# Two last mixers: matmuls on constants ahead of the first turned head, and VectorE's maximum of the next head ahead of the division

## The chip, the cores and the metric

The kernel runs on one NeuronCore of a Trainium2 chip. Its engines work side by side: TensorE (PE) multiplies, with weight loads shown apart (PEld), VectorE (DVE) and ScalarE (ACT) work elementwise, GpSimd (POOL) does some of that too and issues a few transfers, and SyncE (SP) issues the rest. The metric is the device time of one launch in microseconds (us). The time before is 1626.62 us, the median of three runs (1623.18 to 1626.62). The execution that was profiled took 1630.73 us, and its span from the first to the last instruction is 1628.8 us.

## The reference, cut to what matters

The program is two residual blocks on 256 tokens of width 1024, in float32. The first block has feed-forward parts and two mixers. The second block has two layers, and each is one mixer. These two are the "last mixers".

```python
for l in range(2):                                   # second_block
    h = rms_norm(x, norm_g[l])
    q_a, k_a, v_a, q_h, f_h, i_h, q_m, z = split(h @ w_in[l])
    o_a = moba_attention(qa, ka, va)                 # 8 heads of 64, causal over 256 keys
    o_h = rms_norm(hgrn2_chunkwise(q_h, f_h, i_h))   # 4 heads of 128
    o_m = memory_attention(qm, km, vm)               # 4 heads of 128, all 256 memory keys
    x = x + concat([o_a, o_h, o_m]) * silu(z) @ w_out[l]
```

For a head, attention is `p = softmax(q k^T * scale)`, then `p v`. With 256 tokens in blocks of 256, the first attention is causal attention inside one block.

## The kernel before, in words

All weights come as panels of 2048 columns. ScalarE writes the upper part of a panel (L1499), VectorE the rest (L1814), and TensorE multiplies the parts in three products, which together keep float32's accuracy. Small products of activations (attention, norms) are plain float32 products.

The order of the work is not found by a scheduler. `order()` writes one list of steps, each with its engine, and every engine takes its own steps from that list in that order; each step starts with the semaphore waits that it needs. An engine never passes a step that waits. `merge` lays several chains of rounds side by side: round i of the list is round i of each chain, in the order of the chains. `rounds(steps, units)` makes a chain in which, in round r, each step works on the unit r minus its lag. `weave` puts panel products between rounds; in the attention rounds no panels are left, so that TensorE has only attention there.

`last_mixer(l)` is one of the two last mixers. Its attention chain has 12 heads: moba 0 to 7, then matt 0 to 3 (the memory heads). One head goes through seven steps:

1. `scores`, PE L1409 and L1411: q times k into a bank of PSUM. The moba heads have 64 channels, so these products use 64 rows of the array (64\*128 in a row of the profile); matt heads use 128.
2. `mask_max`, DVE L2101 (moba) or L2099 (matt): adds the mask, copies to `probs` (in `work`), finds the row maximum. It waits for `scores` of its head, and for `turn_p` two heads back, whose buffer it takes.
3. `exp`, ACT L1708 twice, each with a row that reads the sum.
4. `divide`, DVE L2114 and L2118: one over the sum, times the probabilities.
5. `turn_p`, PE L1421, L1422, L1427 (matt: L1424, L1425): transposes of 128 columns; waits for `divide`.
6. `p_cols`, ACT L1719: copies the transposed probabilities out of PSUM.
7. `attend`, PE L1367 and L1368: v times the probabilities.

In round r TensorE does `turn_p` of head r-2, `scores` of head r, `attend` of head r-3. ScalarE does `p_cols` of head r-2 and `exp` of head r. VectorE does, by the table `ATTEND`, `divide` of head r-1 and then `mask_max` of head r. A second table, `ATTEND_TWO`, is used by the attention of the first block's second mixer and has the two VectorE steps the other way round.

Rounds 0 and 1 also hold the last norms: L1396 is a product with a matrix of ones, L1697 and L1698 on ScalarE make the reciprocal root from it, L2065 on VectorE applies it. In the first of the two mixers ScalarE also computes row statistics of the memory input in round 5 (L1540 to L1548) and VectorE scales it (L1892). In the second, every other round from 2 to 8 has four transposes more (L1221). `y_splits` and the output panels follow.

Semaphores of `pe_done`, `act_done` and `dve_done` count finished steps; steps named in `UNCOUNTED` don't count.

Of the kernel before, what the change touches and what calls it, by code (L numbers as in the profile page):

```python
# [165 lines left out]
DOWNS = list(RESIDUALS.values())  # L166

LATE = {name: (BASE[name] + N_OF[name] + SLOTS - 1, min(BASE[name] + N_OF[name] + SLOTS, PANELS)) for name in DOWNS}
UNCOUNTED = {"half", "half_hi", "half_lo", "gate_first", "up_first", "first_hi", "first_lo", "ffn_down", "logs", "split_hi", "split_lo", "ffn", "panel", "load", "store"}
PAIRS = DC // 2  # L170

# [4 lines left out]
def rounds(steps, units):  # L177

    return [[(engine, kind, (units[r - lag],)) for engine, kind, lag in steps if 0 <= r - lag < len(units)]
            for r in range(len(units) + max(lag for _, _, lag in steps))]  # L180
# [6 lines left out]
def merge(*chains):  # L187

    return [sum((c[i] for c in chains if i < len(c)), []) for i in range(max(map(len, chains)))]

def weave(chain, pieces, places):

    out, rest = [], []
    pieces = sorted(zip(places, range(len(pieces)), pieces))
    for i, r in enumerate(chain):
        out += r + rest
        rest = []
        while pieces and pieces[0][0] <= i:  # L200
            out += rest
            first, *rest = pieces.pop(0)[2]
            out.append(first)
    return out + rest + sum((p[2] for p in pieces), [])

def halves(panels):

    out, late = [], []  # L210
    panels = panels[:-2] + [p[:2] for p in panels[-2:]]
    for (_, _, args), *rest in panels:
        now = [half_split(s, 0) if s[1] in HALVED else s for s in rest]
        out += [[("pe", "half", (*args, 0)), *late], [("pe", "half", (*args, 1)), *now]]
        late = [half_split(s, 1) for s in rest if s[1] in HALVED]
    out[-1] += late
    return out
# [5 lines left out]
def half_split(step, part):  # L223
# [7 lines left out]
ATTEND = [("pe", "turn_p", 2), ("pe", "scores", 0), ("pe", "attend", 3), ("act", "p_cols", 2), ("dve", "divide", 1),  # L231
          ("dve", "mask_max", 0), ("act", "exp", 0)]

ATTEND_TWO = ATTEND[:4] + [ATTEND[5], ATTEND[4], ATTEND[6]]
# [23 lines left out]
def square_sums(tag):  # L258

    return [("pool", "add", (tag, b)) for b in range(1, PAIRS)]  # L260
# [37 lines left out]
def panel_list(name, extra=None, start=0, stop=None):  # L298

    all_ = []  # L300
    for k in range(start, N_OF[name] if stop is None else stop):
        out = []
        all_.append(out)
        n = BASE[name] + k
        out.append(("pe", "panel", (name, k)))
        if not name.startswith("out"):
            out.append(("dve" if (name, k) in EVACUATED_BY_DVE else "act", "evacuate", (name, k)))
        late = LATE.get(name, (0, 0))
        if n + SLOTS < PANELS and not late[0] <= n + SLOTS < late[1]:

            out += splits(n + SLOTS)[:1 if n + SLOTS == late[0] - 1 else 2]
        out += (extra or {}).get(k, [])
    return all_
# [25 lines left out]
def ffn_steps(f):  # L339
    tag = f"ffn{f}"  # L340
    return norm_steps(tag) + ([("pe", "up_first", (f,)), ("pe", "norm_sum", (tag,))] if f == 0 else
                              [("pe", "gate_first", (f, b)) for b in range(PAIRS)] + [("pe", "norm_sum", (tag,)), ("pe", "up_first", (f,))]) + [("pe", "ffn", (f,)), ("act", "rstd", (tag,)), ("act", "ffn", (f,)), ("dve", "ffn", (f,))]
# [32 lines left out]
def hgrn_rounds(l):  # L375

    out = [[("dve", "f_abs", (l,)), ("act", "f_ln", (l,))], [("dve", "f_log", (l,))]]
    if l:
        out += [[("act", "f_ln2", (l,)), ("dve", "f_log2", (l,))]]
    out += [[("act", "k_gate", (l,)), ("dve", "cum_f", (l,))], [("pe", "diagonal", (l,)), ("dve", "diagonal_in", (l,))]]  # L380
    ahead = len(out)
    for r in range(8 + 2):
        out.append([(e, k, (l, v)) for e, k, v in
                    [("dve", "gap_f", r), ("act", "decay_f", r), ("dve", "q_level", r - 1), ("pool", "k_level", r - 1),
                     ("pe", "level", r - 2), ("dve", "level_in", r - 2)] if 0 <= v < 8])
    return out + [[("pe", "hgrn_out", (l, g)) for g in (0, 1)]], ahead

def last_mixer(l):

    hgrn, ahead = hgrn_rounds(l)
    hgrn[ahead + 9] += [("act", "silu", (f"in2_{l}", 15)), ("act", "logs", ())]
    n = ahead + 9
    qk = [(f"mq{l}", 0), (f"mk{l}", 0), (f"mq{l}", 1), (f"mk{l}", 1)]
    h = n + 7
    chains = [rounds(NORM_COLS, [(f"sk{l}", 0), (f"sk{l}", 1)]), hgrn,
              [[]] * n + rounds(NORM_COLS, qk + [(f"ho{l}", 0), (f"ho{l}", 1), (f"sq{l}", 0), (f"sq{l}", 1)]),
              [[]] * (n + 2) + rounds(ROPE, qk),
              [[]] * (h + 11) + [[("dve", "gate_out", ((f"moba{l}", g),)) for g in (0, 1)]],
              [[]] * h + rounds(ATTEND, [(f"moba{l}", i) for i in range(8)] + [(f"matt{l}", i) for i in range(4)]),  # L400
              [[]] * (h + 13) + [y_splits(l, 0), y_splits(l, 2)]]
    if l == 0:
        load, *stats = mem_norm(1)
        chains += [[[]] * (h + 1) + [[load]] + [[]] * 3 + [[s for s in stats if s[0] == "act"]] +
                   [[s for s in stats if s[1] == "scale"]]]
    if l:
        chains += [[[]] * (h + 2) + sum(([[("pe", "turn_back", (b,)), ("act", "rows_back", (b,))], []] for b in range(PAIRS)), [])]
    places = [n + r for r in BESIDE_2]
    out = weave(merge(*chains), halves(panel_list(f"in2_{l}", None, 4)), places)
    return (out + late_splits(f"in2_{l}") + [("dve", "gate_out", ((f"matt{l}", g),)) for g in (0, 1)]  # L410
            + y_splits(l, 8) + y_splits(l, 10))

def late_splits(name):

    n = BASE[name] + N_OF[name]
    return splits(n + 1, n + 2)

def y_splits(l, b):  # L420
    return [("act", "y_hi", (l, b)), ("dve", "y_lo", (l, b))]
# [10 lines left out]
def mem_norm(l):  # L432

    tag = f"mem{l}"
    return [("pool", "load", (tag,))] + row_stats(tag, 0) + row_stats(tag, 1) + \
        [("dve", "scale", (tag, t)) for t in (0, 1)] + [("pe", "turn_x", (tag, b)) for b in range(PAIRS)]
# [11 lines left out]
def order():  # L448
# [8 lines left out]
    out += square_sums("ffn0") + [("pool", "load", ("tab1",)), ("act", "wab_hi", ()), ("dve", "wab_lo", ())]  # L457
    out += [s for s in ffn_steps(0) if s[1] in UNCOUNTED or s[1] in ("norm_sum", "rstd")] + ffn_tail(0, "mix0")

# [62 lines left out]
for _e, _k, _a in ORDER:  # L522
    if _k not in UNCOUNTED:
        _counts[_e] = _counts.get(_e, 0) + 1
# [4 lines left out]
def at(engine, kind, *args):  # L529

    return COUNT_AT[engine, kind, args]

def build(nc, x_in, mem_in, pos_in, panels, gains, small_in, tab0, tab1, tab2, tab3, out):
    with ExitStack() as ctx:
        def sb(name, shape, dt=F32):
            return ctx.enter_context(nc.sbuf_tensor(name, shape, dt))

        def sem(name):
            return ctx.enter_context(nc.semaphore(name))  # L540
# [14 lines left out]
        const = sb("const", [P, tab0.shape[1]])  # L555
# [6 lines left out]
        ps = ctx.enter_context(nc.psum_tensor("ps", [P, 8, 512], F32))  # L562
# [6 lines left out]
        def cst(name):  # L569
            a, n = PLACES[0][name]  # L570
            return const[:, a:a + n]
# [104 lines left out]
        pe_done, act_done, dve_done, pool_done = (done[e] for e in ("pe", "act", "dve", "pool"))  # L676
# [6 lines left out]
        first_hi, first_lo = sem("first_hi"), sem("first_lo")  # L683
# [30 lines left out]
        for g in range(2):  # L714
            s2 = slice(2 * g, 2 * g + 2)
            s4 = slice(4 + 2 * g, 6 + 2 * g)
            ones, ones64 = cst("ones"), cst("ones64")
# [285 lines left out]
        def _(pe):  # L1003
# [426 lines left out]
            def attend(unit):  # L1430
# [7 lines left out]
                p = p_t[:, i % 2]  # L1438
                weighted(o, v[:, 0], v[:, 1], p[:, 0:SEQ], p[:, SEQ:512] if full else p[:, SEQ:384], full).then_inc(pe_done, 1)

            def lam_sum():
                pe.wait_ge(dve_done, at("dve", "lam_mul"))
                pe.matmul(ps[:, 3, 0:2], cst("ones")[0:64, :], lam_c[0:64, 0:2], start=True, stop=True).then_inc(pe_done, 1)
# [20 lines left out]
            def hgrn_out(l, g):  # L1464
                pe.wait_ge(dve_done, at("dve", "level_in", l, 7))
                for i in range(2):
# [10 lines left out]
                         "turn_m": turn_m, "kq": kq, "double_y": double_y, "double": double, "u": u, "state": state_mm,  # L1477
                         "from_state": from_state, "delta_out": delta_out, "ret_scores": ret_scores, "ret_out": ret_out,
                         "swap": swap, "cn_sum": cn_sum, "scores": scores, "turn_p": turn_p, "attend": attend,
                         "lam_sum": lam_sum, "diagonal": diagonal, "level": level, "hgrn_out": hgrn_out})  # L1480

        @block.scalar
# [831 lines left out]
```

## Time and profile before

| | us |
|---|---|
| median of three runs | 1626.62 |
| the profiled execution | 1630.73 |
| its span | 1628.8 |
| TensorE busy | 1552.1 (95% of the span) |
| VectorE busy | 1177.2 (72%) |
| ScalarE busy | 769.3 (47%) |
| chain that ended last: PE, DVE, ACT | 78%, 13%, 6% |

### The profile page before, as it was taken

The numbers are of one execution on the slowest core, as the hardware profiler recorded it, in microseconds if no ns is written. First come the engines' busy times: TensorE is split into PE (matmuls) and PEld (weight loads), VectorE is DVE, ScalarE is ACT, GpSimd is POOL, SyncE is SP. The second block draws the span as 40 slices with busy tenths as digits, with TensorE's granted clock in tenths as the row PEclk, the third lists the DMA queues.
The fourth block names the chain that finished last, engine by engine and source line by source line (L and its number), as shares of the span: only waits on it lengthen the run. The fifth ranks groups of instructions, "written<-read, shape, count | busy, mean of one in ns | idle before, by whom it ended". The sixth has DMA issues, their size and how long they took to land.

```text
span 1628.8 us, 23944 instructions
## 1 busy us (share of the span) xinstructions
PE 1552.1 (95%) x9974; PEld 1380.3 (85%) x9974; DVE 1177.2 (72%) x1391; ACT 769.3 (47%) x943; POOL 94.3 (6%) x66
## 2 busy tenths in 40 slices
PE   7999998998999999999998999999999899899998
PEld 6888898887888888888987888888999579799757
DVE  7888667636887788786676787867787565589644
ACT  5433545325433454335535534355656554554643
POOL 1000000010000000000000100001031001012000
PEclk9999989999999999999999999999999799999969
DMA  7555533204555545555421555544543124434202
GB/s 275 194 197 181 180 128 132 78 27 160 202 186 185 184 174 193 195 181 181 181 104 68 214 184 186 192 169 151 181 156 119 63 104 168 144 130 148 86 1 78
DMA packets 51888, 246.76 MB, mean 151 GB/s; under 512 B 4619, under 2 KB 5771, under 8 KB 27718
## 3 DMA queue, kind: packets, MB, share of 16 engines
q1 hardware_dynamic: 50662, 238.29, 41.2%
q0 software_dynamic: 1120, 6.96, 1.2%
q8 instruction: 79, 1.29, 0.3%
q14 instruction: 27, 0.22, 0.0%
HBM read 244.18 MB, written 1.05 MB: 151 GB/s over the span
## 4 chain that ended last, share of the span: by engine, by line
PE 78%; DVE 13%; ACT 6%; issue 3%; DMA 0%; SPq 0%; DVEq 0%; POOL 0%; ACTq 0%
PE ps L1055 19%; PE ps L1057 10%; PE ps L1006 9%; PE ps L1007 9%; PE ps L1008 9%; PE ps L1107 7%; PE ps L1252 4%; PE ps L1108 4%; DVE w_lo L1814 3%; ACT w_hi L1499 2%; DVE act_two L1920 1%; PE ps L1367 1%; PE ps L1396 1%; PE ps L1411 1%; ACT act_two L1577 1%
## 5 line engine op out<-in xcount | busy, mean ns | idle before, releaser
L1499 ACT ACTIVATE w_hi<-raw 128x2048 fp32r<-128x2048 f32 x188 | 359.2, 1914 | 390.3 <-PE ps L1057 278.3
L1814 DVE TENSOR_TENSOR w_lo<-raw,w_hi 128x2048 fp32r<-128x2048 f32 x188 | 437.2, 2331 | 144.4 <-ACT w_hi L1499 141.4
L1055 PE MATMUL ps<-act_two,w_hi 128*128 128x512 f32 x1408 | 445.1, 398 | 5.0 <-DVE w_lo L1814 2.4
L1006 PE MATMUL ps<-act_two,w_hi 128*128 128x256 f32 x1120 | 329.7, 294 | 16.8 <-DVE act_two L1920 5.4
L1007 PE MATMUL ps<-act_two,w_hi 128*128 128x256 f32 x1120 | 320.2, 286 | 0.0
L1008 PE MATMUL ps<-act_two,w_lo 128*128 128x256 f32 x1120 | 320.2, 286 | 0.0
L1057 PEld LDWEIGHTS ps<-act_two,w_lo 128*128 128x128 f32 x1408 | 265.9, 189 | 63.1
L1057 PE MATMUL ps<-act_two,w_lo 128*128 128x256 f32 x1408 | 277.8, 279 | 0.0
L1006 PEld LDWEIGHTS ps<-act_two,w_hi 128*128 128x128 f32 x1120 | 218.3, 195 | 23.5 <-issue 7.8
L1055 PEld LDWEIGHTS ps<-act_two,w_hi 128*128 128x128 f32 x1408 | 215.4, 189 | 8.0 <-DVE w_lo L1814 3.6
L1007 PEld LDWEIGHTS ps<-act_two,w_hi 128*128 128x128 f32 x1120 | 218.3, 195 | 3.2 <-issue 3.1
L1008 PEld LDWEIGHTS ps<-act_two,w_lo 128*128 128x128 f32 x1120 | 218.2, 195 | 0.0
L1107 PE MATMUL ps<-g_two,w_hi 128*128 128x512 f32 x384 | 135.6, 396 | 0.0
L1107 PE MATMUL ps<-act_two,w_hi 128*128 128x512 f32 x320 | 112.9, 397 | 2.8 <-DVE act_two L1853 2.8
L1797 DVE TENSOR_TENSOR w_lo<-raw,w_hi 128x1024 fp32r<-128x1024 f32 x72 | 99.0, 1403 | 21.7 <-ACT w_hi L1508 20.5
L1006 PE MATMUL ps<-w_hi,act_two 128*128 128x256 f32 (+1 forms) x336 | 107.7, 321 | 0.0
L1108 PE MATMUL ps<-g_two,w_lo 128*128 128x256 f32 x384 | 107.1, 279 | 0.0
L1007 PE MATMUL ps<-w_lo,act_two 128*128 128x256 f32 (+1 forms) x336 | 101.5, 302 | 0.0
L1008 PE MATMUL ps<-w_hi,act_two 128*128 128x256 f32 (+1 forms) x336 | 101.5, 302 | 0.0
L990 POOL TENSOR_TENSOR pair<-pair 128x512 f32<-128x512 f32 x27 | 41.2, 1528 | 872.9 <-ACT pair L1556 872.2
L1108 PE MATMUL ps<-act_two,w_lo 128*128 128x256 f32 x320 | 89.3, 279 | 0.0
L1107 PEld LDWEIGHTS ps<-g_two,w_hi 128*128 128x128 f32 x384 | 72.1, 188 | 16.6
(282 smaller groups left out, 2079.0 us busy)
## 6 DMA issues: line engine op xcount, KB each, us to landing
raw<-panels SPq DMA_DIRECT2D x184, 1024.0 KB, 4.8
raw<-panels SPq DMA_DIRECT2D x80, 512.0 KB, 4.8
raw<-panels SPq DMA_DIRECT2D x8, 256.0 KB, 5.7
table<-tab POOLq DMA_DIRECT2D x1, 1472.0 KB, 9.4
table<-tab POOLq DMA_DIRECT2D x1, 1216.0 KB, 5.5
xn<-x_in SPq DMA_DIRECT2D x4, 256.0 KB, 4.8
work<-mem_in POOLq DMA_DIRECT2D x1, 1024.0 KB, 9.3
xn<-mem_in POOLq DMA_DIRECT2D x1, 1024.0 KB, 5.2
```

The lines of the kernel that those rows point to most:

```text
L990: nc.gpsimd.tensor_tensor(pair[:, 0:512], pair[:, 0:512], pair[:, 512 * b:512 * b + 512], ALU.add).then_inc(pool_done, 1)
L1006: pe.matmul(o, l[0], r[0], start=start, stop=False, skip_group_check=shared)
L1007: pe.matmul(o, l[0], r[1], start=False, stop=False, skip_group_check=shared)
L1008: return pe.matmul(o, l[1], r[0], start=False, stop=stop, skip_group_check=shared)
L1055: pe.matmul(grid(ps[:, bank + half], 2), w[half][0], act_two[:, slots[c]], start=c == 0, stop=False)
L1057: ins = pe.matmul(ps[:, bank + half, 0:SEQ], w[half][1], act_hi[:, slots[c]], start=False, stop=c == DC - 1)
L1107: pe.matmul(grid(ps[:, bank], 2), hi, two, start=first and m == 0, stop=False)
L1108: ins = pe.matmul(ps[:, bank, 0:SEQ], lo, two[:, 0], start=False, stop=last and m == len(quarters) - 1)
L1252: ins = pe.transpose(oh, lhs(h), ident) if turn else pe.matmul(oh, lhs(h), rhs(h), start=True, stop=True)
L1499: nc.scalar.activation(w_hi[:, s], raw[:, s], ACT.Copy).then_inc(panel_hi, 1)
L1797: ins = tt(w_lo[:, s, c], raw[:, s, c], w_hi[:, s, c].bitcast(F32), ALU.subtract)
L1814: tt(w_lo[:, s], raw[:, s], w_hi[:, s].bitcast(F32), ALU.subtract).then_inc(panel_lo, 1)
```

## The change

Two things are changed in `last_mixer`, so in both last mixers.

The attention rounds take `ATTEND_TWO` in place of `ATTEND`. On VectorE, `mask_max` of head r now stands ahead of `divide` of head r-1.

A new TensorE step `keep_busy(l, 14)` stands at the end of round 1, behind `scores` of moba 1 and ahead of `turn_p` of moba 0. It waits for the rope of the last keys, which has read bank 3 of PSUM, and then multiplies a matrix of ones with 384 columns of constants 14 times into bank 3. Nobody reads the result, and the step has no semaphore of its own.

```diff
-UNCOUNTED = {"half", "half_hi", ...
+UNCOUNTED = {"keep_busy", "half", "half_hi", ...
@@ last_mixer(l)
-              [[]] * h + rounds(ATTEND, [(f"moba{l}", i) for i in range(8)] + [(f"matt{l}", i) for i in range(4)]),
-              [[]] * (h + 13) + [y_splits(l, 0), y_splits(l, 2)]]
+              [[]] * h + rounds(ATTEND_TWO, [(f"moba{l}", i) for i in range(8)] + [(f"matt{l}", i) for i in range(4)]),
+              [[]] * (h + 13) + [y_splits(l, 0), y_splits(l, 2)],
+              [[]] * (h + 1) + [[("pe", "keep_busy", (l, 14))]]]
@@ the steps of TensorE
+            def keep_busy(l, n):
+
+                pe.wait_ge(dve_done, at("dve", "rope", (f"mk{l}", 1)))
+                for _ in range(n):
+                    pe.matmul(ps[:, 3, 0:384], cst("ones"), const[:, 0:384], start=True, stop=True)
```

TensorE in the first last mixer, from the norm product of round 1 on. Before:

```order
L1396 MATMUL ps<-pair,const 128x512
L1409 MATMUL ps<-work 128x128
L1411 MATMUL ps<-work 128x256
L1421 MATMUL ps<-const,work 128x128
L1422 MATMUL ps<-const,work 128x128
L1427 MATMUL ps<-const,work 128x128
L1409 MATMUL ps<-work 128x128
L1411 MATMUL ps<-work 128x256
```

The same place in the changed kernel, whose lines are 1 higher up to L1441 of before and 7 higher behind it:

```order
L1397 MATMUL ps<-pair,const 128x512
L1410 MATMUL ps<-work 128x128
L1412 MATMUL ps<-work 128x256
L1446 MATMUL ps<-const 128x384 x14
L1422 MATMUL ps<-const,work 128x128
L1423 MATMUL ps<-const,work 128x128
L1428 MATMUL ps<-const,work 128x128
L1410 MATMUL ps<-work 128x128
L1412 MATMUL ps<-work 128x256
```

The 14 products (L1446) have come between the scores of head 1 and the three transposes of head 0; nothing else has moved on TensorE.

VectorE in the first last mixer, from the norm of round 1 on: the division of head 0 (L2114, L2118) and the maximum of head 1 (L2101, with the rows that read its result), then the same for the next pair. Before:

```order
L2065 SCALAR_TENSOR_TENSOR work<-work,small,pair 128x512
L2114 RECIPROCAL stat<-stat 128x2
L2118 TENSOR_SCALAR work<-work,stat 128x128
L2118 TENSOR_SCALAR work<-work,stat 128x256
L2101 ISA work,stat<-ps,table 128x128
L2101 ISA stat 128x1
L2101 ISA work,stat<-ps,table 128x256
L2101 ISA stat 128x1
L2114 RECIPROCAL stat<-stat 128x2
```

The same place now:

```order
L2072 SCALAR_TENSOR_TENSOR work<-work,small,pair 128x512
L2108 ISA work,stat<-ps,table 128x128
L2108 ISA stat 128x1
L2108 ISA work,stat<-ps,table 128x256
L2108 ISA stat 128x1
L2121 RECIPROCAL stat<-stat 128x2
L2125 TENSOR_SCALAR work<-work,stat 128x128
L2125 TENSOR_SCALAR work<-work,stat 128x256
L2108 ISA work,stat<-ps,table 128x128
```

The maximum of head r has moved in front of the division of head r-1, in every round of both mixers. ScalarE's order is as it was.

## Rows read from the trace of the kernel before

**Rows 1.** The profile page: TensorE's granted clock in 40 slices, in tenths.
```profile
PEclk9999989999999999999999999999999799999969
```

**Rows 2.** Stretch table: length, busy PE, PEld, DVE, ACT, POOL, granted clock, DMA.
```profile
1278.43:1283.47 5.04, 0.15 (x1) 0.00 (x0) 1.80 (x7) 2.79 (x7) 0.00 (x0) 0.67 0.47 185
1289.95:1305.49 15.54, 15.54 (x45) 8.70 (x44) 6.32 (x27) 9.29 (x32) 0.00 (x0) 0.50 0.00 1
1305.49:1308.59 3.10, 3.10 (x12) 2.18 (x12) 1.86 (x10) 1.48 (x5) 0.00 (x0) 0.68 0.00 0
857.00:863.60 6.60, 6.33 (x27) 5.17 (x28) 4.25 (x16) 4.30 (x14) 0.00 (x0) 0.50 0.20 82
877.65:881.15 3.50, 1.86 (x11) 1.56 (x11) 2.02 (x12) 2.37 (x8) 0.00 (x0) 1.00 0.00 0
1556.88:1574.11 17.23, 17.23 (x53) 10.41 (x53) 5.44 (x28) 7.11 (x23) 0.00 (x0) 0.50 0.00 1
```

**Rows 3.** Timeline, first mixer, where TensorE stands idle: start, length, engine, line.
```profile
1277.99 0.59 PE L1411 MATMUL ps<-work 64*128 64x256 f32 x2
1281.88 0.75 DVE L2065 SCALAR_TENSOR_TENSOR work<-work,small,pair 128x512 f32<-128x512 f32 x1 [3.13 <-ACT pair L1698]
1282.67 0.17 DVE L2114 RECIPROCAL stat<-stat 128x2 f32<-128x2 f32 x1
1283.47 0.47 PE L1421 MATMUL ps<-const,work 128*128 128x128 f32 x1 [4.89 <-DVE work L2118]
```

**Rows 4.** Timeline of TensorE: two fp32 products of 512 columns at full clock.
```profile
1252.71 1.02 PE L1396 MATMUL ps<-pair,const 128*128 128x512 f32 x2
1253.57 1.02 PE L1385 MATMUL ps<-work,table 128*128 128x512 f32 x2
```

**Rows 5.** Timeline, first mixer: one round of an early head at half clock.
```profile
1289.95 0.48 PE L1421 MATMUL ps<-const,work 128*128 128x128 f32 x1
1290.50 0.17 DVE L2114 RECIPROCAL stat<-stat 128x2 f32<-128x2 f32 x1 [1.17 <-ACTq L1711]
1290.70 0.55 DVE L2118 TENSOR_SCALAR work<-work,stat 128x128 f32<-128x128 f32 x2
1292.36 1.11 PE L1367 MATMUL ps<-work 128*64 128x256 f32 x2
1292.56 0.29 DVE L2101 CUSTOM_DVE_ANT_0 work<-ps,table 128x128 f32<-128x128 f32 x1 [1.32 <-issue]
```

**Rows 6.** Timeline, layer 1 mixer of the first block: one round at full clock.
```profile
877.65 0.33 PE L1421 MATMUL ps<-const,work 128*128 128x128 f32 x1 [1.65 <-DVE work L2118]
878.69 0.59 PE L1367 MATMUL ps<-work 128*128 128x256 f32 x2
878.99 0.29 DVE L2101 CUSTOM_DVE_ANT_0 work<-ps,table 128x128 f32<-128x128 f32 x1 [1.39 <-PE ps L1411]
881.15 0.33 PE L1421 MATMUL ps<-const,work 128*128 128x128 f32 x1 [1.65 <-DVE work L2118]
```

**Rows 7.** Timeline, first mixer: the last heads, at full clock.
```profile
1313.90 0.33 PE L1421 MATMUL ps<-const,work 128*128 128x128 f32 x1 [0.59 <-DVE work L2118]
1314.82 0.59 PE L1411 MATMUL ps<-work 128*128 128x256 f32 x2
1317.81 0.51 ACT L1708 ACTIVATE work<-work,stat 128x256 f32<-128x256 f32 x1 [1.25 <-DVE work L2099]
1320.11 0.33 PE L1421 MATMUL ps<-const,work 128*128 128x128 f32 x1 [1.45 <-DVE work L2118]
```

**Rows 8.** Timeline of ScalarE, first mixer: the row statistics, first and last.
```profile
1298.23 0.63 ACT L1540 ACTIVATE work<-xn 128x512 f32<-128x512 f32 x1
1303.09 0.20 ACT L1548 ACTIVATE stat<-stat 128x1 f32<-128x1 f32 x1
```

**Rows 9.** Timeline of TensorE, second mixer: the first and last turned head.
```profile
1549.74 0.48 PE L1421 MATMUL ps<-const,work 128*128 128x128 f32 x1 [4.89 <-DVE work L2118]
1588.68 0.33 PE L1421 MATMUL ps<-const,work 128*128 128x128 f32 x1 [1.26 <-DVE work L2118]
```

More of the change, by code:

```diff
@@ L168 @@
 LATE = {name: (BASE[name] + N_OF[name] + SLOTS - 1, min(BASE[name] + N_OF[name] + SLOTS, PANELS)) for name in DOWNS}
-UNCOUNTED = {"half", "half_hi", "half_lo", "gate_first", "up_first", "first_hi", "first_lo", "ffn_down", "logs", "split_hi", "split_lo", "ffn", "panel", "load", "store"}
+UNCOUNTED = {"keep_busy", "half", "half_hi", "half_lo", "gate_first", "up_first", "first_hi", "first_lo", "ffn_down", "logs", "split_hi", "split_lo", "ffn", "panel", "load", "store"}
 PAIRS = DC // 2
@@ L1479, in _ @@
                          "swap": swap, "cn_sum": cn_sum, "scores": scores, "turn_p": turn_p, "attend": attend,
-                         "lam_sum": lam_sum, "diagonal": diagonal, "level": level, "hgrn_out": hgrn_out})
+                         "lam_sum": lam_sum, "keep_busy": keep_busy, "diagonal": diagonal, "level": level, "hgrn_out": hgrn_out})
         @block.scalar
```

## The prediction

> **What bounds the kernel now.** I read the granted clock of the page first. Two slices near the ends of the layers fall to 7 tenths and 6 tenths [rows 1]; these are the attention rounds of the two last mixers. Then the table by stretch. In the first mixer TensorE stands idle in 1278.43:1283.47 (0.15 us busy of 5.04) and the mean clock of that stretch is 0.67, so that it falls in there. It stays at 0.50 for the four rounds of 1289.95:1305.49, in which TensorE has no idle time at all, and comes back inside 1305.49:1308.59 [rows 2]. The second mixer does the same: idle for 4.89 us up to 1549.74 [rows 9], 0.50 in the four rounds of 1556.88:1574.11 [rows 2]. Outside these holes TensorE is the bound, and all that follows a mixer waits for it, so each us won or lost here is one of the total.
>
> Third, the timeline says why TensorE idles. The scores of head 1 start their last product at 1277.99. The first transpose waits for the division of head 0, which waits on VectorE behind the norm L2065 at 1281.88, which waits for ScalarE's norm (3.13 us) [rows 3]. I call the starts of L1421 turns T0 to T11, one per head. In the first mixer T0 is 1283.47, T2 1289.95, T6 1305.49, T7 1308.59, T11 1320.11.
>
> **The constants.** A float32 product of 512 columns takes 1253.57 - 1252.71 = 0.86 us at full clock [rows 4], so 384 columns take 0.645 and 14 of them 9.03 us. They start when the scores of head 1 are through: 1277.99 + 0.43 (256 columns) = 1278.42. They end at 1287.45. T0 was 1283.47, so they run 4.0 us past the hole that they fill. The hole of the second mixer has the same length, so T0 is late by 4.0 there too. Bounds for the 14: the row shows two records for one product; were only one of them needed, the 14 would take 4.5 us, VectorE would set the end (below) and T0 be late by 0.65. If they ran at half clock they would take 18 us and T0 be late by 13. I take 9.03, as the row is a product of the same type and the same size of weights, at full clock. Their wait, for a rope long done, costs nothing.
>
> In the meantime VectorE does the maximum of head 1 (0.68, from 1282.67) and then divides head 0 (0.75: 1290.50 to 1290.70 + 0.55 [rows 5]), so T0 could be at 1284.15. The 0.65 us by which the new order alone makes T0 late is hidden by the constants; without them it would show.
>
> **The new order of VectorE.** Before, a head's exp, division and the next maximum were a loop. Now the maximum of head r is made while exp works on head r-1. But it has to wait for the scores of head r, and these stand on TensorE behind turn r-2. So the new loop is turn, scores, maximum, division, next turn. At half clock: turn and scores 1292.36 - 1289.95 = 2.41, to VectorE's start 0.20, maximum 0.68, division 0.75, to the next turn 0.05: 4.1 us [rows 5]. Before, four rounds took 15.54 us [rows 2], 3.9 each, bound by TensorE. At full clock: 1.04 for turn and scores, 0.30 to VectorE [rows 6], and again 0.68 + 0.75 + 0.05: 2.8 us. The first block's mixer, which has this order already, confirms the loop: its round in rows 6 is 3.50 us, and it has one multiplication of 0.68 more in front of its division. So the reorder costs 0.2 a round where the clock is low and it cannot get a round under 2.8 where it is high.
>
> **Does the clock hold?** This decides the size. The constants keep TensorE at work from 1278.4 to 1287.5, so it is at full clock when the turns begin. What comes then is a round with a turn and scores but no attend, and then rounds of 2.8 us in which TensorE has about 1.7 us of work (1.04 of rows 6, and 0.65 for an attend of as many columns as the scores) and idles for the rest. The nearest rows speak both ways. For holding: the round of rows 6 (1.86 us busy of 3.50) stays at 1.00 [rows 2]. Against: in that round all products use 128 rows, while a moba head's scores use 64 [rows 3]. And in 1289.95:1305.49 TensorE was busy without a gap with exactly these turns, scores and attends, and the clock did not come back; panel products brought it back within 857.00:863.60, and it came back in the very round in which the first 128-row scores stand [rows 2]. So the moba rounds weigh little, and at full clock they fill only 60% of the time, less than they did while the clock stayed low. Just ahead of the fall TensorE also had 64-row scores and one norm product, and then nothing. I take it that the clock falls again, 2.5 to 6 us behind the constants, in both mixers.
>
> **The sum.** Turns of the first mixer: T0 +4.0. T0 to T2 was 6.48 and is now one full round and one in between (2.8 + 3.45 = 6.25): -0.2. T2 to T6, four rounds at half clock: 16.4 against 15.54: +0.85. T6 to T11, with matt scores of twice 256 columns: T6 to T7 was 3.10; the loop (scores end later, maximum 0.82, division 0.75) makes it 4.2. The next is 3.2, and two rounds at full clock are each 1315.25 - 1313.90 = 1.35 to the end of the scores, + 0.30 + 0.82 + 0.85 = 3.3 [rows 7]; VectorE's two times are for 256 columns, estimated from the 0.68 and 0.75 above. The last turn gains: its maximum and exp are made early, so that it follows the one before by 2.30 (1317.81 to 1320.11 [rows 7]) less 0.86 of lead, 1.45. Together 4.2 + 3.2 + 6.6 + 1.45 = 15.5 against 14.62: +0.9. First mixer: +5.5.
>
> Second mixer: T0 +4.0; T0 to T2 was 7.14, is 6.25: -0.9; T2 to T6 was 17.23 [rows 2], of which two rounds carry four transposes more and stay bound by TensorE, the other two +0.2 each: +0.4; T6 to T11 was 1588.68 - 1574.11 = 14.57 and is 15.5: +0.9. Second mixer: +4.4. Sum +9.9 us on the profiled execution's 1630.73, whose span is 1628.8. The median is 4 us below that execution, and the difference carries over: 1626.62 + 9.9 = 1636.5.
>
> **Rivals.** (a) The clock holds in both mixers. Then T0 to T6 is six rounds of 2.8. In the first mixer ScalarE's row statistics (1298.23 to 1303.29, 5.0 us [rows 8]) stand between the exps of heads 5 and 6 and no longer hide: +2.0. T6 = 1287.45 + 16.8 + 2.0 = 1306.3, then 3.2 + 3.2 + 6.6 + 1.45: T11 = 1320.8, +0.6. In the second: 1553.7 + 16.8 + 14.45 = 1585.0, -3.7. Sum -3.1: 1623.5. For it speaks the 1.00 of rows 6's round; against it the half-height scores. The Trainium skill, in "TensorE: Matmul & The Clock Gate", section "Why this matters for your kernels", advises that no long idle gap be left between bursts of matmuls if the clock is to stay up. By that rule alone this rival would come true, since the changed kernel leaves only short gaps; no run here shows yet whether short gaps between small products suffice, and the four half-clock rounds without any gap make me doubt it.
> (b) The clock holds in one mixer or falls several rounds later. Each round spared saves 1.3 us of loop and up to 2 in the second mixer: the total is then near 1631.
> (c) The change works as a wait only: the constants are at full clock, but the fall comes at once when they end, and then T0 to T2 is 8 us. That is +1.8 and +1.0 more: 1639. It decides the sign by itself from the point where the constants outlast the hole by more than the rounds give back.
> (d) The constants are cheap, the change is the reorder alone: the clock falls in the hole as before, +0.65 + 0.85 + 0.9 and +0.65 + 0.4 + 0.9: about +4, 1631.
>
> **How the numbers follow.** Forecast 0.6, (a) 0.14, (b) 0.12, (c) 0.1, (d) 0.04. The likeliest's own range is 1632 to 1641 (the place of the fall, +-1.5 a mixer, and the loop's length). The range for 8 in 10 takes in most of (b) and a part of (a): 1625.5 to 1641.5. About 0.2%, 3.3 us, is what a measurement of this kernel can tell from no change: faster needs 1623.3 or less, half of (a) with its uncertainty, 0.08. Within 0.2% are the other half and a third of (b): 0.14. Slower: 0.78.
>
> **What would show it.** L1446's 14 products at 0.64 us each, from 1278.4 to 1287.5, clock 1.00 over them; then a fall to 0.50 within two or three turns and a rise again with the matt scores. Turns 2.8 us apart at full clock and 4.1 at half, with VectorE's maximum always right behind the scores and its division right behind the maximum. T11 at 1326 in the first mixer. I am wrong if the granted clock is 1.00 through the turns of either mixer, or if turns at full clock come under 2.6 us apart, which would mean that the scores do not stand in the loop.

## The result, and the profile after

The changed kernel takes 1631.61 us (median of nine runs, 1629.36 to 1635.96), the kernel before 1625.02 in the same comparison (nine runs, 1621.44 to 1627.66). The ratio is 1.0043, with a 95% interval of 1.0029 to 1.0056: 7.0 us slower, 4.7 to 9.1. The profiled execution of the changed kernel took 1633.33 us. Its granted clock, against [rows 1]:

```profile
span 1631.4 us, 24056 instructions
PEclk9999999999999999999998999999999899999999
```

The slice of the first last mixer has gone from 7 to 8 tenths, that of the second from 6 to 9. So the constants did what they are named for in one mixer, and yet the time rose. The table by stretch of the changed kernel says where (length, busy PE, PEld, DVE, ACT, POOL, granted clock, DMA):

```profile
1286.99:1291.00 4.01, 2.39 (x15) 1.59 (x13) 1.36 (x7) 1.94 (x6) 0.00 (x0) 0.99 0.00 0
1291.00:1311.50 20.50, 19.75 (x56) 11.15 (x55) 8.31 (x37) 11.37 (x40) 0.00 (x0) 0.50 0.00 0
1549.04:1558.69 9.65, 9.65 (x32) 5.56 (x31) 2.83 (x13) 3.78 (x11) 0.00 (x0) 1.00 0.00 0
1558.69:1561.91 3.22, 1.93 (x12) 1.19 (x10) 1.45 (x7) 1.29 (x5) 0.00 (x0) 1.00 0.01 3
1561.91:1576.98 15.07, 12.12 (x63) 7.29 (x64) 6.80 (x35) 8.85 (x30) 0.00 (x0) 1.00 0.00 1
```

In the first mixer the first turn (transposes of head 0) comes at 1286.99, and 4.0 us later the clock is at 0.50, for 20.5 us. In the second the same 9.65 us pass between the scores of head 1 and the first turn, and the clock then stays at 1.00 through all turns (the last two rows above show it up to T6). The timeline of the first mixer answers to [rows 3]: VectorE has long divided head 0 when the constants end.

```profile
1277.34 0.59 PE L1412 MATMUL ps<-work 64*128 64x256 f32 x2
1277.86 9.30 PE L1446 MATMUL ps<-const 128*128 128x384 f32 x28
1282.01 0.29 DVE L2108 CUSTOM_DVE_ANT_0 work<-ps,table 128x128 f32<-128x128 f32 x1
1282.69 0.17 DVE L2121 RECIPROCAL stat<-stat 128x2 f32<-128x2 f32 x1
1286.99 0.27 PE L1422 MATMUL ps<-const,work 128*128 128x128 f32 x1
```

The 14 products run from 1277.86 to 1286.99, 9.13 us; the division starts at 1282.69, so that head 0 waits some 3.5 us for nothing. One round of the second mixer, at full clock, answers to [rows 6]:

```profile
1561.91 0.33 PE L1422 MATMUL ps<-const,work 128*128 128x128 f32 x1 [1.29 <-DVE work L2125]
1563.24 0.65 PE L1368 MATMUL ps<-work 128*64 128x256 f32 x2
1563.44 0.29 DVE L2108 CUSTOM_DVE_ANT_0 work<-ps,table 128x128 f32<-128x128 f32 x1 [1.58 <-PE ps L1412]
1564.12 0.17 DVE L2121 RECIPROCAL stat<-stat 128x2 f32<-128x2 f32 x1
1564.93 0.33 PE L1422 MATMUL ps<-const,work 128*128 128x128 f32 x1 [0.82 <-DVE work L2125]
```

Turn, scores, maximum, division, turn: 3.02 us. TensorE idles before each turn until the division is done. The line L1368 is the first product of `attend`, so its start marks where the scores end.

To compare mixers I count from the start of the last scores product of head 1, so that what happened earlier in the launch falls out. T0 and T11 are the first and last turns, counted in us from that point. The eleven numbers behind them are the distances from each turn to the next. All are differences of starts in the timelines of TensorE:

```
kernel, mixer        T0     T11    distances
before, 1           5.48  42.12   2.60 3.88 3.88 3.88 3.88 3.90 3.10 2.40 2.91 3.29 2.92
before, 2           5.48  44.42   3.32 3.82 4.79 3.83 4.79 3.82 4.05 2.08 2.42 3.29 2.73
after, 1            9.65  47.59   2.96 3.27 4.10 4.10 4.10 4.10 4.03 3.21 3.32 3.32 1.43
after, 2            9.65  42.31   3.22 3.02 3.01 3.01 3.02 3.01 3.15 3.21 3.32 3.33 1.36
```

From the last turn of one mixer to the scores of the next, 224.1 us pass in both kernels, and 40.1 from the last turn of the second to the end. What the change does lies in the mixers alone. The stretch ahead of them, whose code is the same, has no fixed length: over the twelve profiled runs of this document the scores of head 1 start between 1272.29 and 1281.38 us. On the whole the later starts go with more time at half clock on the way there, 17 to 38 us in all (from the granted clock read in steps of 1 us). So one profiled run can differ from another by more than this change is worth before the changed code begins.

### The profile page after: what moved, and what is told of

Its sections match the earlier page's. It is cut to its first block, busy times and chain, and to the rows that moved or that the text cites. A ratio compares the mean times of both kernels' runs of the same rounds, so it can differ in the third digit from the quotient of the medians.

```text
span 1631.4 us, 24056 instructions
## 1 busy us (share of the span) xinstructions
PE 1556.9 (95%) x10030; PEld 1381.7 (85%) x10030; DVE 1177.0 (72%) x1391; ACT 768.2 (47%) x943; POOL 94.3 (6%) x66
## 4 chain that ended last, share of the span: by engine, by line
PE 77%; DVE 13%; ACT 4%; issue 3%; DVEq 0%; POOL 0%; ACTq 0%
PE ps L1056 18%; PE ps L1058 9%; PE ps L1007 9%; PE ps L1009 9%; PE ps L1008 9%; PE ps L1108 7%; PE ps L1253 4%; PE ps L1109 4%; DVE w_lo L1821 3%; ACT w_hi L1506 2%; DVE act_two L1927 1%; PE ps L1446 1%; PE ps L1397 1%; PE ps L1412 1%; ACT act_two L1584 1%
```

## The experiments

**The kernel before, once more.** The ratio says 7 us, but the two profiles differ by 2.6. No edit, one profiled run.

> The kernel before, looked at once more. Theory A (the first profile was an execution with a longer stretch at half clock than most): the stretches at half clock in the two last mixers are shorter by 3 to 7 us each, the turns before and after them are the same, the time is 1622 to 1627 us. Rival: stretches as in the first profile (27.3 and 30.7 us), and the difference lies ahead of the last mixers.

It took 1624.42 us. First mixer: T11 at 42.08, as in the first profile. Second: T11 at 42.02 in place of 44.42, since the clock came back after 23.9 us and not 30.7. The half-clock stretch of this run ends inside the second row:

```profile
1545.85:1561.40 15.55, 15.55 (x48) 9.66 (x48) 6.09 (x32) 7.37 (x24) 0.00 (x0) 0.50 0.00 1
1561.40:1582.39 20.99, 18.17 (x86) 12.12 (x84) 11.05 (x47) 11.68 (x37) 0.00 (x0) 0.88 0.00 1
```

The rest of the difference lies ahead of the last mixers: the scores of head 1 start at 1274.18 and not at 1277.99, with less time at half clock near 212 us (3.4 against 10.2). So each expectation was half right. The first profile is of an execution near the slow end of its kernel, and times should be compared by medians, stretches by counting from a point inside.

**The changed kernel, once more.** No edit, one profiled run.

> The changed kernel, looked at once more. Theory A (where the clock falls behind the constants is decided anew in each run): the two mixers need not do as in the first profile; a mixer in which it holds has turns 3.0 us apart, T11 at 42.3 us from the last scores product of head 1 in the second mixer and about 44 in the first (with ScalarE's row statistics in the way), one in which it falls has 4.1 between turns. Rival D (something in the first mixer alone makes it fall, each time): it falls in the first and holds in the second again.

It took 1632.87 us. Its stretches:

```profile
1284.91:1287.90 2.99, 1.37 (x9) 0.81 (x7) 1.36 (x7) 1.33 (x5) 0.00 (x0) 1.00 0.00 0
1287.90:1311.80 23.90, 23.16 (x65) 13.06 (x66) 9.05 (x41) 11.97 (x42) 0.00 (x0) 0.50 0.00 0
1561.00:1567.80 6.80, 6.50 (x22) 3.98 (x20) 2.71 (x14) 2.76 (x10) 0.00 (x0) 0.50 0.00 0
1567.80:1590.88 23.08, 18.14 (x95) 11.73 (x93) 12.41 (x54) 12.81 (x39) 0.00 (x0) 1.00 0.01 1
```

The first mixer fell 3 us behind the constants (T11 at 48.70), the second fell too, but for 6.8 us only (T11 at 44.30). So whether and where the clock falls differs from run to run. The mean clock of the changed kernel's nine runs also splits them, though it doesn't say in which mixer the clock fell: four at 0.980 to 0.983 take 1631.6 to 1636.0 us, five at 0.986 to 0.988 take 1629.4 to 1632.2. Even the second group is slower than the median before.

With two profiled runs of each kernel, T11 moves by +5.5 and +6.6 us in the first mixer and by nothing on average in the second (42.31 and 44.30 against 44.42 and 42.02). That makes 6 of the 7 us. Two runs of each are few, so this is a match in size and not a proof.

**The two halves apart.** The new order alone:

```diff
-              [[]] * (h + 13) + [y_splits(l, 0), y_splits(l, 2)],
-              [[]] * (h + 1) + [[("pe", "keep_busy", (l, 14))]]]
+              [[]] * (h + 13) + [y_splits(l, 0), y_splits(l, 2)]]
```

> Maximum ahead of the division in both last mixers, no constants. Turns are counted from the start of the last scores product of head 1 (5.48 us to T0 and 42.1 us to T11 before, in the first mixer). Theory A (the reorder costs by itself: its loop goes through the scores): the clock falls in the hole as before, T0 comes 0.65 us later, rounds at half clock are 4.1 us in place of 3.9, the last turns cost 0.9 more: about +2 us a mixer, +4 in all. Rival B (the reorder is what pays or is free, and the constants carry the whole loss): 0 or less.

1634.61 us against 1626.25: ratio 1.0058 (1.004 to 1.0077), 9 us slower, where +4 was expected. The sign went to theory A. The size was missed in the first two rounds:

```profile
1282.86 0.47 PE L1421 MATMUL ps<-const,work 128*128 128x128 f32 x1 [5.57 <-DVE work L2124]
1285.47 0.29 DVE L2107 CUSTOM_DVE_ANT_0 work<-ps,table 128x128 f32<-128x128 f32 x1 [2.67 <-PE ps L1411]
1286.15 0.17 DVE L2120 RECIPROCAL stat<-stat 128x2 f32<-128x2 f32 x1
1286.95 0.48 PE L1421 MATMUL ps<-const,work 128*128 128x128 f32 x1 [1.62 <-DVE work L2124]
```

At half clock the new loop is 4.10 us in each of the first six rounds of the first mixer, also in the first two, which took 2.60 and 3.88 before, as no attend bounds them yet. In the second mixer the first two take 4.35 and 4.10, where they took 3.32 and 3.82. T0 is at 6.17, 0.69 later. T11 is at 46.15 and 45.81: +4.0 and +1.4 against the first profile of before, +4.1 and +3.8 against the second. On average that is 6.6 us; where the other 2 to 3 us of the measured 9 lie, the profiled run doesn't show.

The constants alone:

```diff
-              [[]] * h + rounds(ATTEND_TWO, ...
+              [[]] * h + rounds(ATTEND, ...
```

> The 14 products of constants, with the old order of VectorE. T0 is 4.2 us late in both mixers as in the changed kernel. Theory A: where the clock holds, rounds are bound by exp, division, maximum (2.6 us, as the first round before the change) and not by 3.0; so this is 2 to 4 us faster than the changed kernel in each mixer where the clock holds, and 2 faster where it falls (rounds of 3.9, the cheaper tail). Against before: near 0 with the clock held in both, +4 if it falls in one. Rival B: slower than the changed kernel, since the reorder is lost.

1623.92 us: ratio 0.9985 (0.9972 to 0.9998), 2.4 faster than before. T0 is at 9.65, but the turns that follow are 1.27, 2.82, 2.60, 2.60, 2.60 us apart in the first mixer, and 1.77, then 2.3 to 2.6 in the second. One such round:

```profile
1288.28 0.33 PE L1422 MATMUL ps<-const,work 128*128 128x128 f32 x1 [0.63 <-DVE work L2125]
1288.94 0.40 ACT L1715 ACTIVATE work<-work,stat 128x128 f32<-128x128 f32 x1 [0.94 <-DVE stat L2108]
1290.07 0.17 DVE L2121 RECIPROCAL stat<-stat 128x2 f32<-128x2 f32 x1 [1.17 <-ACTq L1718]
1290.86 0.29 DVE L2108 CUSTOM_DVE_ANT_0 work<-ps,table 128x128 f32<-128x128 f32 x1
1290.88 0.33 PE L1422 MATMUL ps<-const,work 128*128 128x128 f32 x1 [0.41 <-DVE work L2125]
```

The loop of the old order is exp, division, maximum: 2.60 us at full clock against 3.01 with the new order. T11 is at 42.55 and 38.54. In the first mixer the clock held up to ScalarE's row statistics, where one turn came 6.42 us after the one before and the clock fell for some 3.4 us. In the second it held throughout:

```profile
1550.85:1579.74 28.89, 24.52 (x133) 16.20 (x131) 15.79 (x72) 17.96 (x55) 0.00 (x0) 1.00 0.00 1
```

That makes a clean pair. The second mixer of the changed kernel's first profile also has T0 at 9.65 and the clock at 1.00 through all turns, and its T11 is at 42.31. The two differ by the order on VectorE alone, with the clock out of play, and the new order costs 3.8 us there.

**Fewer constants.** With the new order, and with the old:

```diff
-              [[]] * (h + 1) + [[("pe", "keep_busy", (l, 14))]]]
+              [[]] * (h + 1) + [[("pe", "keep_busy", (l, 8))]]]
```

> The changed kernel with 8 products of constants in place of 14: 5.2 us, which is the length of the hole. Theory A: T0 is only 0.65 us late (set by VectorE's new order), 3.5 us a mixer better than the changed kernel, as long as the clock holds as there: 7 us faster in all, about as fast as before or up to 4 faster. If the clock falls in both mixers, as in the kernel before: +4 against before, as the reorder alone. Rival C (the constants' length does not cost, since the engines behind are the bound): equal to the changed kernel.

1630.18 us, ratio 1.0029 (1.0016 to 1.0042): 4.7 slower than before, and some 2 faster than the changed kernel, not 7. The two intervals overlap, so even the 2 are not sure. T0 is at 6.16 as expected, 3.5 us earlier. But the clock falls in the first mixer behind the second turn, in the second mixer for 6.8 us from 1561.0, and T11 is at 44.14 and 41.04:

```profile
1291.40:1311.80 20.40, 19.66 (x57) 11.03 (x56) 8.31 (x37) 11.56 (x40) 0.00 (x0) 0.50 0.00 0
1561.00:1567.80 6.80, 6.06 (x22) 3.70 (x20) 2.32 (x12) 3.10 (x11) 0.00 (x0) 0.50 0.00 0
```

The comparison with the changed kernel goes over two sets of runs and is only as good as their common kernel before. Trace and medians don't agree well here. By the two T11 together this profiled run is 6.3 us better than the changed kernel's two on average, near the 7 expected, and level with before (85.2 against 86.5 and 84.1). The median is 4.7 above before all the same. The profiled run is one of the slowest (1632.64), and it is late ahead of the mixers, with the scores of head 1 at 1281.38. What makes the other runs slow stays open. Rival C fell in the trace, where 3.5 us of T0 come off in each mixer; the medians confirm it in the pair with the old order, below.

> 8 products of constants with the old order of VectorE. Theory A: T0 as before (+0.1), rounds of 2.6 us at full clock where it holds. If it holds in both mixers: first mixer about -3, second about -8 against before, 10 us faster in all; if it falls in both behind the constants: -2. Rival C: equal to the constants alone with 14.

1617.93 us, ratio 0.9956 (0.9941 to 0.9972): 7.2 faster than before. T0 at 5.79, T11 at 39.85 and 35.51, turns 2.6 us apart; the clock held but for 6.8 us behind the row statistics in the first mixer:

```profile
1280.97:1297.90 16.93, 11.50 (x59) 6.76 (x57) 7.86 (x38) 11.12 (x39) 0.00 (x0) 1.00 0.00 0
1297.90:1304.70 6.80, 6.19 (x18) 3.85 (x19) 3.60 (x15) 4.26 (x15) 0.00 (x0) 0.50 0.00 0
```

Against the 14 with the old order the eight are 4.8 us faster, and the intervals (0.9941 to 0.9972, 0.9972 to 0.9998) no more than touch. With the new order the same eight constants give 12 us less. This pair differs by the reorder alone, the fall of the clock that came with it included (it fell in both mixers with the new order, in one with the old), and it is the largest single effect of the study. The other two pairs say nearly the same: the new order costs 9 us without constants, and 9 with 14 of them (+7.0 against -2.4).

**Does the clock fall because the rounds are thin?** One more product in each of the rounds 2 to 8 of the first mixer, in a bank that is free there:

```diff
-              [[]] * (h + 1) + [[("pe", "keep_busy", (l, 14))]]]
+              [[]] * (h + 1) + [[("pe", "keep_busy", (l, 14))]] + [[("pe", "keep_busy", (l, 1))]] * (0 if l else 7)]
-                    pe.matmul(ps[:, 3, 0:384], cst("ones"), ...
+                    pe.matmul(ps[:, 3 if n > 1 else 5, 0:384], cst("ones"), ...
```

> The changed kernel, and in the first mixer one product of constants (0.65 us) more at the end of each of the rounds 2 to 8, where TensorE waits for the division at full clock. Theory A (the clock falls there because the rounds behind the constants hold too little work): it holds in the first mixer in nearly all runs, turns stay 3.0 us apart but for the 5 us of row statistics, T11 at 43 to 45 us in place of 47.6; 3 us faster than the changed kernel at its lower clock, and the runs no longer fall into two groups. Rival F (the fall has another cause, or one more product delays each turn): the clock falls as before and the first mixer takes 4 us more.

```profile
1284.09:1300.80 16.71, 15.63 (x69) 8.25 (x67) 7.55 (x36) 9.59 (x32) 0.00 (x0) 1.00 0.00 0
1300.80:1318.26 17.46, 13.34 (x63) 8.27 (x63) 10.45 (x41) 10.25 (x33) 0.00 (x0) 1.00 0.00 1
```

The clock holds from the first turn to the last. Turns are 3.01 apart, one of 4.72 carries the row statistics, and T11 is at 43.83 in place of 47.6 and 48.7. In the second mixer, which has no such products, it held too (T11 at 42.30). The mean clock of all seven runs is 0.985 to 0.990: one group, where the changed kernel had two. 1628.92 us, ratio 1.0037 (1.0021 to 1.0052), against 1.0043 for the changed kernel. The 3 us that were expected between the two can't be told from none.

So in the profiled run more work in those rounds went with a clock that stayed up, at no cost to the turns, and the kernel is still slower than before. With the clock at full level through both mixers, T0 is late by 4.2 us and the loop is the longer one. That explains only a part: T11 of the two mixers together is 0.8 us later than in the two profiles of before on average, while the ratio says 6 us. The profiled run is the fastest of its seven (1626.65), and what the others lost is not shown.

**The row statistics.** Eight constants, old order, ScalarE's six steps in six rounds:

```diff
-        chains += [[[]] * (h + 1) + [[load]] + [[]] * 3 + [[s for s in stats if s[0] == "act"]] +
-                   [[s for s in stats if s[1] == "scale"]]]
+        a, d = [s for s in stats if s[0] == "act"], [s for s in stats if s[1] == "scale"]
+        chains += [[[]] * (h + 1) + [[load]] + [[]] * 3 +
+                   [[a[0]], [a[1]], [a[2]], [a[3], d[0]], [a[4]], [a[5]], [d[1]]]]
```

> Eight constants and the old order, and in the first mixer ScalarE's row statistics are spread over the rounds 5 to 10, a step each, in place of one block behind the exp of head 5. Theory A: the turn that took 6.42 us takes 2.6 to 3.4, some 3 us less with 0.5 to 1 given back in the later rounds, and the clock no longer falls behind it: 2 to 4 us faster than the eight constants with the block, 10 to 12 faster than before. Rival E (ScalarE's work is only moved and each round grows by it, since exp is in the loop): the same time as with the block.

1612.5 us, ratio 0.9937 (0.9916 to 0.9958): 10 us faster than before, as expected, and 3 more than with the block, though the intervals overlap. The eight runs fall into two groups: five at 1609.6 to 1612.9 us with mean clock 0.989 to 0.992, three at 1618.8 to 1619.6 with 0.980 to 0.982. The profile is of the second group: the clock fell at 1286.0, 4.0 us behind the first turn, and T11 of the first mixer is at 40.94. The turn that took 6.42 us takes 3.88, at half clock.

```profile
1282.00:1286.00 4.00, 3.05 (x17) 1.90 (x16) 1.68 (x9) 2.46 (x9) 0.00 (x0) 1.00 0.00 0
1286.00:1306.50 20.50, 20.45 (x60) 11.49 (x59) 8.85 (x43) 10.47 (x36) 0.00 (x0) 0.50 0.00 0
```

**A version that beats both.** The same with one product more a round in the first mixer (the edit of the thin rounds, with 8 in place of 14):

> Eight constants, old order, row statistics spread, and in the first mixer one product of constants more at the end of each of the rounds 2 to 8. Theory A (the runs of the kernel without these products fall into two groups, near 1612 and near 1619 us, by whether the clock falls behind the eight constants): all runs in the faster group, turns of the first mixer 2.6 us apart, T11 at 36 to 37 us from the last scores product of head 1, median 1609 to 1613. Rival F (the product delays each turn, or the clock falls for another reason): two groups again, or turns 3.2 us apart and 1616.

1611.43 us, ratio 0.9914 (0.9898 to 0.993): 14 us faster than before. All five runs have a mean clock of 0.987 or more, and in the profiled one it is 1.00 in both mixers:

```profile
1279.61:1299.00 19.39, 19.29 (x90) 11.44 (x89) 10.41 (x52) 12.70 (x44) 0.00 (x0) 1.00 0.00 0
1539.67:1569.37 29.70, 24.74 (x133) 16.19 (x131) 16.84 (x77) 18.94 (x59) 0.00 (x0) 1.00 0.00 1
```

Turns of the first mixer are 2.81 apart, also in the rounds ahead of the row statistics, where they were 2.60 without the product. So the product costs 0.2 a round. T11 is at 35.95, and 35.50 in the second. Against the version without it the median hardly moves; what is gone is the group near 1619 us.

Last, the one place where the new order gains:

```diff
+    heads = rounds(ATTEND, [(f"moba{l}", i) for i in range(8)] + [(f"matt{l}", i) for i in range(4)])
+    heads[11].sort(key=lambda s: s[1] == "divide")
```

> The same, and in round 11 alone the maximum of the last head stands ahead of the division of head 10, in both mixers. Theory A (this is the only place where the new order gains, since no scores follow in the loop): the last turn comes 1.4 us after the one before in place of 2.9 and 2.7, the others do not change: 2.8 us faster than the same kernel without it, half of that if head 10's turn is put off. Rival: no difference, as the turn before is late by as much.

1612.31 us, ratio 0.9911 (0.9895 to 0.9927): no difference that can be told. The last turn comes 1.64 and 1.36 us after the one before, in place of 2.92 and 2.72, but the one before is itself later by 0.64. Net 0.6 and 0.7 a mixer in the trace, 1.3 us in all, as the second half of the expectation allowed. The four runs have a mean clock of 0.986 or more.

## Why the prediction was right or wrong

Direction and rough size were right: +9.9 forecast, +7.0 (4.7 to 9.1) measured.

*The constants outlast the hole.* T0 was to be 4.0 us late; it is 4.17 late in both mixers (9.65 against 5.48). The 14 products take 9.13 us against 9.03. The eight of the other runs confirm it: T0 at 5.79.

*The loop through the scores.* At half clock 4.1 forecast, 4.10 measured. At full clock 2.8 forecast, 3.01 measured. The price was taken from a round with 128-row products [rows 6]: turn and scores took 1.04 us there. With 64 rows they take 1.33 (1561.91 to 1563.24), while VectorE starts 0.20 behind and not 0.30. The last rounds: 3.3 and 3.2 forecast, 3.32 and 3.21 measured; the last turn 1.45 forecast, 1.43 measured. So in the first profile the first mixer came out right term by term: from T0 to T2 -0.25 (forecast -0.2), from T2 to T6 +0.86 (+0.85), from T6 to T11 +0.7 (+0.9).

*The fall of the clock.* This is the step that failed in part. "I take it that the clock falls again ... in both mixers" held for the first: it fell 4.0 and 3.0 us behind the constants in the two profiled runs, within the 2.5 to 6 forecast, and the mixer cost +5.5 and +6.6 against +5.5. In the second it held in one run and fell for 6.8 us in the other, so that the mixer cost nothing on average against +4.4. In the run where it held, the four rounds from T2 to T6 took 12.05 us and not 17.2. This is rival (b), which had 0.12 and a time near 1631, some 4.5 us above before. The measured +7.0 lies midway between it and the forecast of +9.9, and that it comes so close is in part luck. The second mixer gave 0 for +4.4, the first gave 0.6 more than forecast, and another 1 us of the 7.0 lies in neither. I had argued from the weight of moba rounds in general. It may be the start that counts, right behind the constants: round 2 has no attend, and in the second mixer that round holds the four transposes L1222 besides. This was not tried by itself, and it isn't enough, since in the changed kernel's second profile the clock fell in the second mixer too, 4.8 us behind the first turn and behind these transposes. What was tried is more products in these rounds. In the three profiled runs that have them the clock is at 1.00 through the first mixer, and none of their 16 runs has a mean clock below 0.985; without them 4 of 9 runs had 0.983 or less (14 constants, new order) and 3 of 8 had 0.982 or less (eight, old order, statistics spread). That the low mean stands for a fall in the first mixer was seen in one profiled run of each of these two kernels, and once more in the changed kernel's second profile; for the other runs it is inferred.

The rule of the Trainium skill ("TensorE: Matmul & The Clock Gate", section "Why this matters for your kernels") is that no long idle gap be left between bursts of matmuls. In the first mixer of the changed kernel TensorE never idles for more than 1.62 us between the constants and the fall, so there keeping to the rule was not enough. In the second mixer the clock held in one profiled run and fell in the other, with idle times of 1.29 us at most between the constants and the fall. The longest idle time of each, in brackets, from the first profile (first mixer) and the second (second mixer):

```profile
1289.95 0.33 PE L1422 MATMUL ps<-const,work 128*128 128x128 f32 x1 [1.62 <-DVE work L2125]
1559.46 0.33 PE L1422 MATMUL ps<-const,work 128*128 128x128 f32 x1 [1.29 <-DVE work L2125]
```

*Rival (a)*, the clock held in both mixers, was to give 1623.5, 3.1 us faster. The profiled run with one product more a round is that case, with T11 at 43.83 and 42.30, and the kernel's ratio is 1.0037: slower. Its T11 in the second mixer was forecast at 40.7 (1585.0 less 1544.26) and came at 42.3, because of the 3.01 in place of 2.8. In the first it was 42.8 and came at 43.8. And the forecast was measured against a profile whose second mixer is 2.4 us slower than in the next one. Against the two profiles of before these two T11 are 0.4 us earlier and 2.0 later together, so the gain of 3.1 isn't there in either comparison.

*Rival (d)*, the reorder alone, was +4; it measured +9. The terms left out were the first two rounds, 1.5 and 0.2 us in the first mixer and 1.0 and 0.3 in the second. The prediction had priced the reorder from T2 to T6 and in the last rounds, and the rounds ahead of T2 only with the clock up. With these 3 us the sum is about 7; the rest has no place in the trace that was found.

## What to carry to other kernels

Work that only keeps TensorE's clock up has to end when the real work is ready: eight products filled this hole, and 14 put the first turn of each mixer 3.5 to 3.9 us later than the eight did. Before moving a step ahead of another on an in-order engine, write down the loop through all engines that results: here the maximum left a loop of 2.6 us and put scores and transposes into one of 3.0 (4.1 at half clock). When a clock falls in some runs and not in others, one profile of each kernel can mislead by as much as the change is worth. Compare medians, profile each kernel twice, and count inside the launch from a common point; then check that what the trace shows adds up to what the medians say. Here it did for the change itself (6 of 7 us) and not for three of the variants (the reorder alone, eight constants with the new order, one more product in each round).

## What the runs showed of the hardware that I had not expected

The granted clock can fall with TensorE idle for no more than 1.62 us at a time (first mixer of the changed kernel), while nearly the same rounds ran at 1.00 in the second mixer of that run. The same program can have its fall in one run and not in the next: the second mixer of the changed kernel stayed at 1.00 in one profiled run and was at 0.50 for 6.8 us in the other. The two groups of the kernel with the statistics spread are 7 us apart (1609.6 to 1612.9 against 1618.8 to 1619.6) and differ in mean clock; only a run of the slower group was profiled. Of the kernel before, 23 runs in one set spread from 1619.32 to 1630.48 us, and their mean granted clock runs the other way, from 0.976 down to 0.968. Products that use 64 rows are not quicker than those of 128: turn and scores took 1.33 us against 1.04 with the same columns, and the scores alone 0.85 (1562.39 to 1563.24 in the changed kernel) against 0.66 (878.03 to 878.69 in the kernel before).
